# Two norms of a transformer block: the token factor applied after the projection instead of before it, the raw residual transposed quarter by quarter, and four instead of five router heads projected ahead

## What is computed

```python
    # end of the first block
    x = x + g2 * conv_ffn(h, ffn_w_gate, ffn_w_up, ffn_conv_w, ffn_conv_b, ffn_w_down)
    return rmsnorm(x, norm_final)
...
    # second block
    h = h + hybrid_mixer(rmsnorm_2(h, attn_norm), w_in, ..., w_out)     # xn @ w_in, attention, @ w_out
    h = h + peer(rmsnorm_2(h, ffn_norm), wq, subkeys, u, v)
    return rmsnorm_2(h, final_norm)
...
def rmsnorm_2(x, g):
    return x * lax.rsqrt(jnp.mean(x * x, axis=-1, keepdims=True) + RMS_EPS) * g
...
def peer(xn, wq, subkeys, u, v):      # 8 heads, 16 experts a head and token
    q = (xt @ wq).reshape(T, PEER_HEADS, 2, PEER_QDIM // 2)
    s1 = einsum('thd,nd->thn', q[:, :, 0], subkeys[0])
    s2 = einsum('thd,nd->thn', q[:, :, 1], subkeys[1])
    # top 16 of each side, top 16 of the sums: idx, gate
    h = gelu(einsum('cd,chkd->chk', xc, u[ic]))
    return einsum('chk,chkd->cd', gc * h, v[ic])
```

## Time and profile before

| | us |
|---|---|
| median of 3 runs | 3637.95 |
| lowest, highest | 3637.66, 3643.27 |
| time of the profiled execution | 3637.52 |
| its span, first to last instruction | 3635.8 |
| busy: PE, DVE, POOL, ACT | 2959.8, 1513.9, 884.4, 447.6 |
| PEld (overlaps PE) | 1787.6 |

### The profile page before, as it was taken

The page is one execution under the profiler, slowest core; times in us unless marked ns, Lnnn a source line. Parts: engine busy times, 40 slices in busy tenths (PEclk is TensorE's granted clock), DMA queues, the critical chain, the costliest instruction groups (busy, mean ns, idle before and its releaser), DMA issues.

```text
span 3635.8 us, 26672 instructions
## 1 busy us (share of the span) xinstructions
PE 2959.8 (81%) x9622; PEld 1787.6 (49%) x9622; DVE 1513.9 (42%) x2323; ACT 447.6 (12%) x992; POOL 884.4 (24%) x633
## 2 busy tenths in 40 slices
PE   5999757989999999996998898777766666656666
PEld 3444636468888884443458764633322222222222
DVE  5663544510000000002014521666677767676665
ACT  1000332020110110001003421010100000110000
POOL 2110100100000000000000000455565656656664
PEclk9999767999999999998997899898888888888888
DMA  9997200834444444444440023989999999999998
GB/s 380 396 401 294 69 0 1 323 128 152 155 154 151 150 150 150 150 150 163 150 143 1 1 71 115 369 361 418 387 409 421 422 421 422 408 422 422 421 422 358
DMA packets 228226, 916.35 MB, mean 252 GB/s; under 512 B 17787, under 2 KB 33331, under 8 KB 156211
## 3 DMA queue, kind: packets, MB, share of 16 engines
q0 software_dynamic: 99840, 637.57, 42.7%
q1 hardware_dynamic: 128037, 277.66, 22.2%
q10 hardware_dynamic: 272, 0.13, 0.0%
HBM read 912.11 MB, written 2.15 MB: 251 GB/s over the span
## 4 chain that ended last, share of the span: by engine, by line
PE 57%; DMA 24%; DVE 10%; POOL 3%; ACT 2%; issue 2%; SPq 0%; DVEq 0%; POOLq 0%; ACTq 0%
PE ps L1138 17%; PE ps L852 14%; DMA arena<-in_peer_v,proj 11%; PE ps L1151 8%; PE ps L1322 5%; DMA proj<-in_peer_u,proj 4%; DMA ring<-in_w_in 3%; DMA proj<-in_peer_v,proj 3%; DMA arena<-in_w_mod 3%; PE ps L1299 3%; POOL arena L461 2%; PE ps L1209 1%; DMA ring<-in_peer_wq 1%; PE ps L1210 1%; DVE proj L1902 1%
## 5 line engine op out<-in xcount | busy, mean ns | idle before, releaser
L1322 PE MATMUL ps<-proj,gates 128*128 128x512 f32 x992 | 572.2, 741 | 370.4 <-DMA proj<-in_peer_v,proj 272.2
L461 POOL DMA_INDIRECT proj<-in_peer_u,proj x128 | 206.9, 1616 | 1776.2 <-DVE proj L1895 1603.1
L1138 PE MATMUL ps<-hT,ring 128*128 128x256 f32 x2816 | 608.0, 379 | 1.5 <-ACT hT L500 1.5
L1322 PEld LDWEIGHTS ps<-proj,gates 128*128 128x128 f32 x992 | 232.6, 242 | 707.4 <-issue 601.1
L1138 PEld LDWEIGHTS ps<-hT,ring 128*128 128x128 f32 x2816 | 535.7, 190 | 73.7 <-issue 1.7
L852 PE MATMUL ps<-ring,hT 128*128 128x512 f32 (+2 forms) x960 | 381.4, 559 | 11.9 <-DMA ring<-in_w_in 11.9
L1902 DVE CUSTOM_DVE_ANT_0 arena<-arena,yT 128x2048 f32<-128x2048 f32 x128 | 291.5, 2291 | 208.8 <-DMA arena<-in_peer_u,proj 208.1
L1902 DVE CUSTOM_DVE_ANT_0 proj<-proj,yT 128x2048 f32<-128x2048 f32 x128 | 292.2, 2292 | 122.9 <-DMA proj<-in_peer_u,proj 119.2
L1151 PE MATMUL ps<-ring,arena 128*128 128x512 f32 x704 | 304.1, 595 | 2.7 <-ACT arena L683 2.7
L852 PEld LDWEIGHTS ps<-ring,hT 128*128 128x128 f32 x960 | 176.2, 195 | 217.5 <-issue 193.1
L1322 PE MATMUL ps<-arena,gates 128*128 128x512 f32 x512 | 234.0, 600 | 37.1 <-DMA arena<-in_peer_v,proj 36.7
(11 more groups left out here) (406 smaller groups left out, 2368.0 us busy)
## 6 DMA issues: line engine op xcount, KB each, us to landing
arena<-in_w_mod POOLq DMA_DIRECT2D x96, 1024.0 KB, 12.4
ring<-in_w_in SPq DMA_DIRECT2D x52, 1024.0 KB, 13.0
ring<-in_ffn_w_gate SPq DMA_DIRECT2D x44, 1024.0 KB, 5.1
ring<-in_ffn_w_up SPq DMA_DIRECT2D x44, 1024.0 KB, 5.1
ring<-in_ffn_w_down SPq DMA_DIRECT2D x44, 1024.0 KB, 4.9
ring<-in_w_out SPq DMA_DIRECT2D x32, 1024.0 KB, 5.7
ring<-in_peer_wq SPq DMA_DIRECT2D x16, 1024.0 KB, 10.9
ring<-in_w_in SPq DMA_DIRECT2D x16, 960.0 KB, 17.0
```

The lines of the kernel that those rows point to most:

```text
L461: pool_eng.indirect_dma_start(row_slots[n % ROWS], None, table, bass.IndirectOffsetOnAxis(expert[:, 0, TOP * g + r:TOP * g + r + 1], 0))\
L1138: ins = pe.matmul(ps[:, 4 * m + f, 0:T], ring[:, s, k, P * f:P * (f + 1)], hT[:, KS * s + k, :], start=(s == 0 and k == 0), stop=(s == SLO ...
L1322: ins = pe.matmul(ps[:, 4 * t + b, :], diag[:, j, :], row_slots[n % ROWS][:, NB * b:NB * (b + 1)], start=(h == 0 and j == 0), stop=(h == H ...
```

## The change

It has six parts.

1. The column quarters of `x` after the feed-forward part are signalled one by one (`x_done` counts 2 to 5). PE transposes each quarter of the raw `x` (`raw_turn`) into the two banks that DVE has just read, ACT multiplies by the column factor on the way to `hT` (`raw_cols`; the weights of both norms are multiplied together once on DVE). The transposes of the first two quarters stand ahead of the first slot of `in2`, those of the other two ahead of the second slot.
2. The token factors of the two norms are computed beside that: DVE keeps the first in `stat[8:10]`, multiplies the second into it, and `evac` of `in2` multiplies each block by the product (ACT for tile 0, DVE for tile 1).
3. SP issues the eight loads for the first two blocks of `in2` ahead of `cmp_w` and `bias` (`in2_loads(0, 2)`), the rest behind them.
4. Before the expert part, the transposes of quarters 0 to 2 of the raw `x` stand inside `out2`, in blocks 1 to 3 behind their first slot; quarter 3 stands in the third slot of head 0. The token factor goes on the scores that `take_head` moves. DVE makes `xs` for the dot products from `x` with one instruction for each tile.
5. The keys are transposed between head 0 and head 1 into bank 0, and their load is issued by ACT ahead of `out2`.
6. `EARLY` is 4 instead of 5: head 4 is projected behind group 0, head 5 behind group 1, and so on.

The diff, without the lines that only load and place the weight row of `norm_final` (one more small load at the start) and the renumbering of two waits:

```diff
@@ -296,3 +296,3 @@
     GS = NT * HEADS
-    EARLY = 5
+    EARLY = 4
     U_ROW = lambda g, r: r if g == 0 else TOP * (2 * g - 1) + 2 * r
@@ -351,2 +351,8 @@
             sp.dma_start(ring[:, b, :, 0:FIRST], w1v["w_in"][:, KS * q:KS * (q + 1), FIRST * b:FIRST * (b + 1)]).then_inc(sem(f"slot{b}"), 16)
+        def in2_loads(first, end):
+            for b in range(first, end):
+                w = min(NB, W2 - NB * b)
+                for q in range(SLOTS):
+                    slot_load(w1v["w_in_2"], (BLK["in2"] + b) * SLOTS, q, False, slice(NB * b, NB * b + w), w)
@@ -388,3 +394,4 @@
                 sp.dma_start(ring[:, s, :, :], wd[:, bass.ds(i, 1), s, :].rearrange("p o (k n) -> p (o k) n", n=NB)).then_inc(sem(f"slot{s}"), 16)
-        sp.wait_ge(*at("x_done", 2))
+        in2_loads(0, 2)
+        sp.wait_ge(*at("x_done", 5))
         for m, name in enumerate(("cmp_w1_k_2", "cmp_w1_v_2")):
@@ -396,4 +403,4 @@
         load("bias_in", hyb["bias"], bass.AP(scratch.tensor, 0, [[1, P], [384, 32], [1, T]]))
-        stream(w1v["w_in_2"], BLK["in2"], 6, W2 - 6 * NB)
-        sp.wait_ge(*at("x_done", 3))
+        in2_loads(2, 7)
+        sp.wait_ge(*at("x_done", 6))
         load("norm_in", gates[:, 0, :], a["ffn_norm_2"].partition_broadcast(P))
@@ -503,3 +510,10 @@
-        def evac(blk, n, dst, tail, tiles=1, col0=0):
+        def raw_cols(n, g, bank, scale):
+            act.wait_ge(*at("hT_turned", 16 + 4 * (n - 2) + g + 1))
+            for k in range(KS):
+                f = KS * g + k
+                ins = act.activation(hT[:, f, :], ps[:, bank + k // 2, T * (k % 2):T * (k % 2 + 1)], ACT.Copy, scale=scale[:, f:f + 1])
+            ins.then_inc(sem("hT_act"), 1)
+        def evac(blk, n, dst, tail, tiles=1, col0=0, scale=None):
@@ -508,3 +522,7 @@
                 pair = 2 * (b % 2)
-                act.copy(dst[:, 0:tiles, cols], ps[:, pair:pair + tiles, 0:w]).then_inc(sem("evac_act"), 1)
+                if scale is None:
+                    ins = act.copy(dst[:, 0:tiles, cols], ps[:, pair:pair + tiles, 0:w])
+                else:
+                    ins = act.activation(dst[:, 0, cols], ps[:, pair, 0:w], ACT.Copy, scale=scale)
+                ins.then_inc(sem("evac_act"), 1)
             with act.Fori(0, n // 2) as i:
@@ -654,3 +672,3 @@
-        def residual_evac(blk, ev):
+        def residual_evac(blk, ev, turned=None):
             for i in range(4):
@@ -660,2 +678,4 @@
                 act.copy(ffn["y"][:, 0, :], ps[:, 2 * (i % 2), :]).then_inc(sem("evac_act"), 1)
+                if turned:
+                    turned(i)
@@ -689,9 +709,10 @@
         act.copy(ffn["act"][:, 0], act_store[:, 4 * (DOWN - 1):4 * DOWN, :]).then_inc(sem("staged"), 1)
-        act.wait_ge(*at("x_done", 2))
+        for g in range(4):
+            raw_cols(2, g, 2 * g, vc("attn_norm", 0, 16))
+        act.wait_ge(*at("x_done", 5))
         norm(2, scaled=False)
-        act.wait_ge(*at("x_done", 3))
-        norm(3)
-        norm_cols(2, vc("attn_norm", 0, 16), None)
-        evac(BLK["in2"], 6, p2, W2 - 6 * NB)
+        act.wait_ge(*at("x_done", 6))
+        norm(3, scaled=False)
+        act.wait_ge(*at("xs_vec", 3))
+        evac(BLK["in2"], 6, p2, W2 - 6 * NB, scale=stat[:, 8:9])
@@ -749,8 +770,8 @@
             head_pair(3, g, False)
-        residual_evac(BLK["out2"], EVB["out2"])
-        act.wait_ge(*at("x_done", 4))
+        act.wait_ge(*at("att_out", 17))
         act.dma_start(peer["keys"], a["peer_subkeys_2"].rearrange("s n d -> n s d")).then_inc(sem("keys_in"), 16)
-        norm(4)
-        norm_cols(3, vc("ffn_norm2", 0, 16), None)
+        residual_evac(BLK["out2"], EVB["out2"], lambda i: raw_cols(3, i, 4 + 2 * (i % 2), vc("ffn_norm2", 0, 16)) if i < 3 else None)
+        raw_cols(3, 3, 6, vc("ffn_norm2", 0, 16))
+        act.wait_ge(*at("x_done", 7))
+        norm(4, scaled=False)
         def best_exp(g):
@@ -779,4 +800,4 @@
             scored = ps[:, pair:pair + 2, T:2 * T].rearrange("p t (s n) -> p t s n", s=2)
-            act.copy(peer["score"][:, h], scored[:, 0]).then_inc(sem("score_out"), 1)
-            act.copy(later[:, 2 * h:2 * h + 2, :], scored[:, 1]).then_inc(sem("later_out"), 1)
+            act.activation(peer["score"][:, h], scored[:, 0], ACT.Copy, scale=stat[:, 6:7]).then_inc(sem("score_out"), 1)
+            act.activation(later[:, 2 * h:2 * h + 2, :], scored[:, 1], ACT.Copy, scale=stat[:, 7:8]).then_inc(sem("later_out"), 1)
@@ -840,6 +861,14 @@
-        def project(lhs, blk, ev, n, tail, by_vec=True):
-            def one(i, step, b, w):
+        def raw_turn(n, g, bank):
+            for k in range(KS):
+                for t in range(NT):
+                    f = KS * g + k
+                    ins = pe.transpose(ps[:, bank + k // 2, T * (k % 2) + P * t:T * (k % 2) + P * (t + 1)], x[:, t, P * f:P * (f + 1)], ident)
+            ins.then_inc(sem("hT_turned"), 1)
+        def project(lhs, blk, ev, n, tail, by_vec=True, begin=None):
+            def one(i, step, b, w, between=None):
                 pe.wait_ge(*at("evac_act", i * step + (ev + b + 1)))
@@ -848,2 +877,4 @@
                 for s in range(SLOTS):
+                    if between:
+                        between(b, s)
                     pe.wait_ge(sem(f"slot{s}"), i * (16 * step) + 16 * (blk + b + 1))
@@ -854,5 +885,11 @@
                     ins.then_inc(sem("unit_used"), 1)
-            with pe.Fori(0, n // 2) as i:
-                one(i, 2, 0, NB)
-                one(i, 2, 1, NB)
+            alone = 0
+            if begin:
+                alone, between = begin
+                for b in range(alone):
+                    one(0, 0, b, NB, between)
+            if alone < n - n % 2:
+                with pe.Fori(alone // 2, n // 2) as i:
+                    one(i, 2, 0, NB)
+                    one(i, 2, 1, NB)
             if n % 2:
@@ -1161,5 +1198,10 @@
-        pe.wait_ge(*at("x_done", 2))
-        norm_turn(2)
-        project(hT, BLK["in2"], EVB["in2"], 6, W2 - 6 * NB)
+        def in2_cols(b, q):
+            if b == 0:
+                for g in ((0, 1), (2, 3), (), ())[q]:
+                    pe.wait_ge(*at("x_done", 2 + g))
+                    raw_turn(2, g, 2 * g)
+                pe.wait_ge(*at("hT_act", 8 + q + 1))
+        project(hT, BLK["in2"], EVB["in2"], 6, W2 - 6 * NB, begin=(2, in2_cols))
@@ -1269,10 +1311,13 @@
         pe.wait_ge(*at("att_out", 17))
-        project(yT, BLK["out2"], EVB["out2"], 4, 0)
-        pe.wait_ge(*at("x_done", 4))
-        norm_turn(3)
-        pe.wait_ge(*at("keys_in", 16))
-        for s in range(2):
-            ins = pe.transpose(ps[:, 7, P * s:P * (s + 1)], peer["keys"][:, s, :], ident)
-        ins.then_inc(sem("keys_turned"), 1)
+        def peer_cols(g):
+            pe.wait_ge(*at("added", 4 + g + 1))
+            if g >= 2:
+                pe.wait_ge(*at("hT_act", 12 + g - 1))
+            raw_turn(3, g, 4 + 2 * (g % 2))
+        def out2_cols(b, q):
+            if b and q == 1:
+                peer_cols(b - 1)
+        project(yT, BLK["out2"], EVB["out2"], 4, 0, begin=(4, out2_cols))
@@ -1288,2 +1333,8 @@
             if h == 1:
+                pe.wait_ge(*at("hT_act", 16))
+                pe.wait_ge(*at("keys_in", 16))
+                pe.wait_ge(*at("evac_act", EVB["out2"] + 2 + 3))
+                for side in range(2):
+                    ins = pe.transpose(ps[:, 0, P * side:P * (side + 1)], peer["keys"][:, side, :], ident)
+                ins.then_inc(sem("keys_turned"), 1)
                 pe.wait_ge(*at("keys_out", 1))
@@ -1293,2 +1344,6 @@
             for s in range(SLOTS):
+                if h == 0:
+                    if s == 2:
+                        peer_cols(3)
+                    pe.wait_ge(*at("hT_act", 12 + (s + 1 if s else 3)))
                 if h % 2 == 0:
@@ -1361,3 +1416,3 @@
-        def evac(blk, n, dst, tail):
+        def evac(blk, n, dst, tail, scale):
@@ -1365,3 +1420,3 @@
                 vec.wait_ge(*at("unit_used", turn + SLOTS * (blk + b + 1)))
-                vec.tensor_copy(dst[:, 1, cols], ps[:, 2 * (b % 2) + 1, 0:w]).then_inc(sem("evac_vec"), 1)
+                vec.tensor_scalar(dst[:, 1, cols], ps[:, 2 * (b % 2) + 1, 0:w], scale, None, ALU.mult).then_inc(sem("evac_vec"), 1)
             with vec.Fori(0, n // 2) as i:
@@ -1733,2 +1788,3 @@
         link.end(11)
+        link(vec.tensor_tensor(vc("attn_norm", 0, 16), vc("attn_norm", 0, 16), vc("norm_final", 0, 16), ALU.mult))
         vec.wait_ge(*at("gate_out", 4))
@@ -1740,6 +1796,8 @@
             link(ins)
-            link(vec.tensor_tensor(x[:, :, r], x[:, :, r], ffn["y2"], ALU.add), "x_done" if n == 3 else None)
+            link(vec.tensor_tensor(x[:, :, r], x[:, :, r], ffn["y2"], ALU.add), "x_done")
         norm(2, scaled=False)
+        vec.tensor_copy(stat[:, 8:10], stat[:, 6:8])
         vec.wait_ge(*at("norm_in", 16))
+        vec.wait_ge(*at("hT_turned", 20))
         for t in range(NT):
@@ -1747,5 +1805,6 @@
         link(ins, "x_done")
-        norm(3)
```

(14 more changed lines are left out.)

10 lines of the change are left out of this document (5 added, 5 removed).

## The result

The changed kernel takes 3597.7 us (median of 4, 3596.5 to 3604.1) against 3637.8 for the kernel before (4 runs on the same chip): a ratio of 0.9889, 95% interval [0.9874, 0.9904], so 35 to 46 us faster. The forecast was 3594.

A forecast was written before the change was run, and what follows sets the result against it. Bounds: at the seam the norm's chain and load queue, almost equal; before the experts PE's norm wait; in the experts the DMA engines. 29 + 7 + 7.5 = 43.5 us off 3637.52 gives 3594.0, range 3585 to 3605.

The forecast's parts named there:

- The seam: Between the blocks, at in2: removing the norm's chain and the load queue from PE's path gains 29 us, between 25 and 31.
- first subtraction: At in2's first block: slow clock after PE's two short idle stretches costs 0 to 2.1 us, taken as 1.
- second subtraction: At in2's block 2: its first slot lands late behind the six other loads; PE waits 0 to 4 us, taken as 1.
- Before the experts: From out2 to the first scores: the choosing of experts starts 7 us earlier, between 4 and 9.
- Four heads ahead: Expert part, head 4 moved behind group 0: 11.5 us of empty DMA time won, 4 lost; gain 7.5, between 0 and 12.
- the dip behind head 4: Expert part: POOL gathers nothing while head 4 passes; queued slots cover most, and 4 us of idle DMA time remain.
- the prediction's own mark: Expert part: the prediction is wrong if the dips behind the four heads sum to more than 15 us.
- The head that costs what it saves: Expert part: head 4 in the loop costs 10 us, leaving 1.5 us of gain there; time 3600; chance 0.14.
- The queue's order biting: At in2's third block: weights late by 8 us, not 1; the seam gains 22 us, time 3601; chance 0.10.
- The whole wait: Expert part: DVE's 21.41 us wait counts, not idle DMA engines; gain there 17 us, time 3584; chance 0.07.
- Nothing gained before the experts: Before the expert part: raw columns start nothing earlier, since head 1 waits for the keys; time 3601; chance 0.04.
- Slower: Expert part: each in-loop head empties the DMA engines for 15.4 us; time 3644; chance 0.03, shared with no change.

The follow-up runs named there:

- eight relatives: The eight other kernels with the changed seam and its order of loads; block 0 is evacuated 38.0 to 38.1 us after the first gated addition.
- old_early4: The kernel before with only EARLY = 4 instead of 5; 3633.0 us, ratio 0.9984 to the kernel before.
- bias_later: The changed kernel, but SP asks for block 2 of in2 ahead of the 4 MB of bias; 3598.2 us, ratio 0.9889 to the kernel before.
- run 1: The changed kernel with five heads ahead of the experts again (EARLY = 5); 3605.2 us, ratio 0.9905 to the kernel before.
- run 3: The changed kernel with the norm, transposes and keys before the experts as they were before; 3607.5 us, ratio 0.9907 to the kernel before.
- queue_old: The changed kernel, but SP issues in2's loads behind the six other loads as before; 3627.2 us, ratio 0.9965 to the kernel before.

## Why the prediction was right, and where it was off

The mechanisms were right, and the time fell 3.7 us above the forecast, inside the range. That it came so close is in part luck. In the two profiles the stages behind the first addition gained 34.7 us and not 43.5: 2.1 are missing at the seam, 0.2 before the experts, 2.8 behind MAX8, and 3.8 went in a stage that the sum has no term for. The stage up to the first addition hides 4.0 of that; it happened to be that much shorter in the profiled execution of the kernel after, and it scatters by 7.6 between kernels.

**The seam, 29 us forecast.** Measured 26.9 at the end of `in2` in this profile (213.90 - 187.01), 26.0 to 26.9 over the six profiles with this code. The term's first subtraction, 1 us for the clock, is the one that was mis-sized: of the raw 30.9 us block 0 kept 28.3, so 2.6 went, and the rows put it on the second quarter's transposes and the first slot (0.9 + 2.3 us over their full-rate durations; 0.45 came back, since the 16 transposes inside the block put it off by 1696.87 - 1695.12 = 1.75 us and not 2.2). In the eight relatives 2.0 to 2.2 went. The bound was 2.1, taken from the first block of before; it had no share for transposes that run slow. The Trainium skill, page "TensorE: Matmul & The Clock Gate", section "HAM oscillation — how this bites in real kernels", tells of bursts of matmuls with waits for loads between them, which return the array to half rate each time. The waits here are shorter than those of its example, and the granted 0.72 behind them agrees with it in direction, against my weighing. The second subtraction, 1 us for the queue, came to 1.48 of wait and 1.8 in all at block 2, within its 0 to 4; in the relatives with that wait it is 1.9 to 3.9. The gain of 26.5 at block 2 becomes 26.9 at the end since the narrow block was 0.35 shorter, by its clock. The factors were hidden, as said.

**What the sum had no term for.** From the end of `in2` to `out2` the kernel before takes 233.6 us (233.61, and 233.59 in `old_early4`, whose code up to there is the same), every other kernel 235.6 to 237.9, with the same instructions. The windows of that stretch, of the kernel before and then of the kernel after, have the reason in the column of the clock:

```profile
1897.20:2130.80 233.60, 203.21 (x1227) 185.80 (x1227) 117.39 (x422) 93.12 (x360) 0.00 (x0) 0.81 0.03 11
```

```profile
1866.20:2103.60 237.40, 206.94 (x1226) 189.30 (x1226) 117.47 (x422) 93.42 (x360) 0.00 (x0) 0.79 0.03 11
```

The same stretch of short matmuls with small gaps is granted 0.81 in the one and 0.79 in the other. Its first group of 32 matmuls, in the timelines of PE of the kernel before and after, took 5.03 and 7.00 us:

```profile
1906.11 5.03 PE L1180 MATMUL ps<-hT,proj 128*128 128x30 f32 x32 [1.88 <-DVE hT L1773]
```

```profile
1875.24 7.00 PE L1222 MATMUL ps<-hT,proj 128*128 128x30 f32 x32 [1.89 <-DVE hT L1832]
```

So 2 to 4 us of the seam's gain were given back behind it. `order_alone`, which changes nothing but the order of loads, shows the same 237.37; so the new code is not needed for it, and a shift in time is the likely cause. What decides the moments at which the clock changes was not tried.

**Before the experts, 7 us forecast.** 6.84 measured, the same in every profile. `out2` grew by 2.6 us and not 3.3, since eight transposes put off the next matmul by 2223.99 - 2223.12 = 0.87 us each time; head 1's wait is 5.13 (5 forecast); the clock behind it cost 1.9 (0 to 2 forecast). Head 0 at full rate is 17.43 x 64/80 = 13.9 us and not the 13.8 of the sum, which changes nothing.

**Four heads ahead, 7.5 us forecast.** 6.0 measured over the profiles, 4.7 in this pair. The removed part was right (12.3 us in windows of 5 us, 11.5 forecast); the 4 us for the dip behind head 4 were too small. It is 6.8 us, and behind head 6 it is 6.4 where the earlier trace rows gave 5. The reasoning that the backlog of eight slots covers most of a POOL stop was right; what I did not see is that the stop's length follows from the 14 us head through ACT's gelu, and that it can be halved. By the prediction's own mark, dips of more than 15 us behind the four heads, it would be wrong: they sum to 6.8 + 0 + 6.4 + 2.4 = 15.6. The mark was badly set, since heads 6 and 7 had dips before the change too and only the difference counts; the gain stood nevertheless.

**The rivals.** The head that costs what it saves (third term 1.5): out, it is 6.0. The queue's order biting for 8 us: out, 1.8, and 3.9 at most in a relative; by the ring-order rule of the Trainium skill, page "DMA: Bandwidth & Descriptors", section "Queues, rings and completion order", the loss was to be 2 us, and `bias_later` agrees, as the wait goes when the bytes ahead go. The whole wait: out by run 1. Nothing gained before the experts: out by run 3. Slower, each in-loop head leaving 15.4 us empty: out, the largest is 6.8.

## What to carry to other kernels

Where two chains end within a few microseconds of each other, price both before removing either: here the columns alone were worth 1 us at the end of `in2` and nothing at block 0, the order of the loads alone 2.5, both together 26.5. In a stage bound by transfers, count the time with nothing queued and not the waits of the engines; and where a long piece of another engine's work causes it, cut the piece in two, so that the stop which it causes (8.49 us instead of 15.38 here) is covered by what is already queued. That was worth 16.7 us, against 6 for moving it. And look at what else stands in line behind the operation that ends a wait: the copy of the keys behind `xs` cost 6.3 us for an order of two instructions.

## What was not expected of the hardware

- The same matmuls and transposes (1226 or 1227 on record) between `in2` and `out2` took 233.6 to 237.9 us, at a mean granted clock of 0.81 in the kernel before and 0.79 in the kernel after and `queue_old`; the kernel before and `old_early4` are alike to 0.02 us. A stage can so change by up to 4 us without any change in it.
- In the narrow block of `in2` PE was busy without a gap, and the granted clock fell to 0.50 even so: the same work took 7.47 to 10.2 us.
- Idle times of 2.83 and 1.43 us around a burst of 1.06 us were followed by a granted clock of 0.72 over 10.7 us of unbroken work.
- Where the DMA share falls below full, the bytes fall further: at a share of 0.92 and 0.74 the engines moved 341 and 267 GB/s of 419. The share alone gives too small a price.
